# Forgetting attention with its rounds written out, four banks for transposed units, and the inverse sums in a score bank

## The reference, cut to what matters

```python
def fox_attention(q, k, v, log_f):
    c = jnp.cumsum(log_f.astype(jnp.float32), axis=1).transpose(0, 2, 1)
    ...
        s = jnp.einsum('bhqd,bhkd->bhqk', qb, kh).astype(jnp.float32) * scale
        s = s + cb[..., :, None] - c[..., None, :]
        mask = key_pos[None, :] <= q_pos[:, None]
        p = jax.nn.softmax(jnp.where(mask, s, -jnp.inf), axis=-1)
        return jnp.einsum('bhqk,bhkd->bhqd', p.astype(vh.dtype), vh)
...
    o_fox = o_fox.astype(x.dtype) * jax.nn.silu(f_gate)
```

## Time and profile before

| | |
|---|---|
| median of three runs | 1271.45 us |
| the profiled execution, its own time | 1274.48 us |
| its span in the profile | 1272.8 us |
| TensorE matmuls busy in the span | 1215.0 us (95%) |
| TensorE weight loads busy | 994.9 us (78%) |
| VectorE, ScalarE, GpSimd busy | 657.2, 547.1, 408.1 us |
| first score matmul of the forgetting stage | 733.87 us |
| first matmul of the output projection | 1088.25 us |

### The profile page before, as it was taken

How to read it: one execution, slowest core, us unless ns; L and a number is a source line. 1 busy time by engine, 2 the same in 40 slices (tenths; PEclk the granted TensorE clock), 3 DMA queues, 4 the chain that set the end, 5 groups by cost and what they waited for, 6 DMA issues and landing times. The chain is left out here.

```text
span 1272.8 us, 18800 instructions
## 1 busy us (share of the span) xinstructions
PE 1215.0 (95%) x6256; PEld 994.9 (78%) x6256; DVE 657.2 (52%) x1472; ACT 547.1 (43%) x1116; POOL 408.1 (32%) x512
## 2 busy tenths in 40 slices
PE   5999999999999999998999979999999998799997
PEld 5998877888777777777888757877787787688886
DVE  3763435101333334422555368878898897544443
ACT  5553033013444442213555357777777777211111
POOL 3554531122333333322334143153126315211110
PEclk9999999999999999999999989999999999899999
DMA  8884232223333334435444493236044201544341
GB/s 317 268 283 128 65 96 96 72 83 115 101 107 107 107 107 132 130 120 154 132 150 141 125 226 124 85 89 154 9 150 108 76 10 45 204 149 149 149 145 70
DMA packets 106819, 161.57 MB, mean 127 GB/s; under 512 B 12148, under 2 KB 62324, under 8 KB 105124
## 3 DMA queue, kind: packets, MB, share of 16 engines
q1 hardware_dynamic: 103920, 151.46, 38.4%
q10 hardware_dynamic: 2616, 8.66, 1.7%
q0 software_dynamic: 192, 0.33, 0.2%
HBM read 102.67 MB, written 57.74 MB: 126 GB/s over the span
## 5 line engine op out<-in xcount | busy, mean ns | idle before, releaser
L1038 PE MATMUL tok_tps<-h_T,tok_slot 128*128 128x512 f32 x2088 | 491.0, 393 | 0.0
L1038 PEld LDWEIGHTS tok_tps<-h_T,tok_slot 128*128 128x128 f32 x2088 | 390.4, 188 | 82.8 <-issue 2.3
L2114 PE MATMUL out_yps<-out_w,out_mix 128*128 128x512 f32 x768 | 177.2, 393 | 8.4 <-POOL out_mix L2163 7.6
L2114 PEld LDWEIGHTS out_yps<-out_w,out_mix 128*128 128x128 f32 x768 | 145.4, 190 | 40.2 <-ACT out_w L2180 8.7
L1875 ACT ACTIVATE fox_pT<-fox_tps 128x512 fp32r<-128x512 f32 x240 | 124.1, 529 | 81.7 <-PE fox_tps L1801 78.1
L1932 DVE TENSOR_TENSOR fox_pT<-fox_tps,fox_pT 128x512 fp32r<-128x512 f32 x240 | 144.3, 606 | 23.2 <-ACT fox_pT L1875 21.3
L1920 DVE TENSOR_SCALAR_CACHE_REDUCE fox_prob<-fox_sps 128x512 f32<-128x512 f32 (+1 forms) x240 | 140.8, 603 | 19.6 <-PE fox_sps L1792 15.8
L1801 PE MATMUL fox_tps<-all_ident,fox_prob 128*128 128x128 f32 x816 | 133.0, 276 | 5.3 <-ACT fox_prob L1867 3.9
L1801 PEld LDWEIGHTS fox_tps<-all_ident,fox_prob 128*128 128x128 f32 x816 | 101.6, 141 | 32.8 <-ACT fox_prob L1867 7.2
L1867 ACT ACTIVATE fox_prob<-fox_prob,fox_nm 128x512 f32<-128x512 f32 (+7 forms) x96 | 114.8, 1196 | 5.3 <-POOL fox_qb L1567 5.3
L1818 PE MATMUL fox_ops<-fox_pT,fox_v 128*128 128x512 f32 (+3 forms) x384 | 111.9, 375 | 2.0 <-ACT fox_pT L1875 2.0
(11 more groups left out here) (199 smaller groups left out, 1661.0 us busy)
## 6 DMA issues: line engine op xcount, KB each, us to landing
scr_split<-cg_stage SPq DMA_DIRECT2D x64, 256.0 KB, 2.9
open_raw<-in_w_cols SPq DMA_DIRECT2D x22, 512.0 KB, 4.3
open_raw<-in_x SPq DMA_DIRECT2D x16, 512.0 KB, 6.9
tok_xT<-in_x_cols SPq DMA_DIRECT2D x16, 512.0 KB, 6.4
scr_gates<-cg_stage SPq DMA_DIRECT2D x32, 256.0 KB, 2.5
outw_mix<-scr_mix SPq DMA_DIRECT2D x16, 512.0 KB, 4.4
out_x<-in_x SPq DMA_DIRECT2D x16, 512.0 KB, 3.5
out<-out_o ACTq DMA_DIRECT2D x15, 512.0 KB, 2.6
```

The lines of the kernel that those rows point to most:

```text
L1038: mm = nc.tensor.matmul(cps[u % 2], w[j % 2][a_][:, kk, :], hT[b_][:, kk, c * CH:(c + 1) * CH], start=(kk == 0 and r == 0), stop=(kk == KT ...
L2114: mm = nc.tensor.matmul(yps[t % 2][:, c, :], mix[t % 2][a][:, kk, :], w[b][:, kk, c * CH:(c + 1) * CH], start=(kk == 0 and n == 0), stop=( ...
```

## The change

The three rounds are written out for all engines, and the loop is gone. There are four `tps` banks, so that transposes of unit n wait for unit n-4. The bank `rps` is gone: the inverse sums are spread into `sps[0]`, the first of the two score banks. With that come two waits on TensorE. The spread waits until the last score unit in that bank, up to the end of the next turn's units, is through VectorE. The first score unit of each turn waits for SCALE of the turn whose sums were spread last (`turn` in the code is the turn being worked on; with its `max(turn - 1, 0)` all turns up to turn-2 must be copied; at turn 0 of a round all those of the round before). The order of work on the engines is otherwise the same.

```diff
-        tps = [k.ps(f"tps{b}", [P, CH]) for b in range(3)]
+        tps = [k.ps(f"tps{b}", [P, CH]) for b in range(4)]
         ops = [k.ps(f"ops{b}", [P, CH]) for b in range(2)]
-        rps = k.ps("rps", [P, CH])
+        rps = sps[0]
...
+        def starts(t):
+            return (t // n_turns) * n_scores + at_turn(t % n_turns)[0]
+
...
-        def rounds(eng, round_):
-            with eng.Fori(0, ROUNDS - 1) as r:
-                round_(r, False)
-            round_(ROUNDS - 1, True)
+        def rounds(round_):
+            for r in range(ROUNDS):
+                round_(r, r == ROUNDS - 1)
...
                         if n >= 2:
                             pe.wait_ge(negated, S.at(n - 1))
+                        if n >= QT and i == QT - 1 and c == 0:
+                            turn = next(x for x in range(n_turns + 2) if starts(x) == n) - 1
+                            pe.wait_ge(scaled, G.at(max(turn - 1, 0)))
...
                     def transposes(u, n, t, q0):
                         e, g, j, i0 = u
-                        pe.wait_ge(pt_lo, K.at(n - 2 if n >= 3 else 0))
+                        pe.wait_ge(pt_lo, K.at(n - 3 if n >= 4 else 0))
...
-                            mm = nc.tensor.transpose(tps[n % 3][:, i * P:(i + 1) * P],
+                            mm = nc.tensor.transpose(tps[n % 4][:, i * P:(i + 1) * P],
...
                         pe.wait_ge(diag_done, G.at(t + 1))
                         pe.wait_ge(scaled, G.at(t))
+                        pe.wait_ge(negated, S.at(starts(min(t + 3, n_turns + (not last))) - 1))
...
-                rounds(pe, round_)
+                rounds(round_)
```

More of the change, by code:

```diff
@@ L1768, in round_ @@
                                 second.load_values(sp, r + 1, 0, 0, NCH)
-                rounds(sp, round_)
+                rounds(round_)
             @block.tensor
@@ L1874, in pt_high @@
                         act.wait_ge(weighed, K.at(max(n - PT + 1, 0)))
-                        nc.scalar.activation(pT[n % PT][HI][:, i0 * P:CH], tps[n % 3][:, i0 * P:CH], ACT.Copy
+                        nc.scalar.activation(pT[n % PT][HI][:, i0 * P:CH], tps[n % 4][:, i0 * P:CH], ACT.Copy
                                              ).then_inc(pt_hi, 1)
@@ L1906, in _ @@
                 act.wait_ge(opening.memory_stored, 8 * ColumnUnits.TURNS)
-                rounds(act, round_)
+                rounds(round_)
             @block.vector
@@ L1931, in pt_low @@
                         dve.wait_ge(pt_hi, K.at(n + 1))
-                        nc.vector.tensor_tensor(pT[n % PT][LO][:, i0 * P:CH], tps[n % 3][:, i0 * P:CH],
+                        nc.vector.tensor_tensor(pT[n % PT][LO][:, i0 * P:CH], tps[n % 4][:, i0 * P:CH],
                                                 pT[n % PT][HI][:, i0 * P:CH].bitcast(F32), ALU.subtract
@@ L1963, in _ @@
                 round_(0, False, prologue=True)
-                rounds(dve, round_)
+                rounds(round_)
             @block.gpsimd
@@ L2015, in round_ @@
                     gated_output(n_turns - 1)
-                rounds(pool, round_)
+                rounds(round_)
     return 8 * ROUNDS * n_turns
```

## The result

The changed kernel takes 1278.29 us in the median of five runs (1277.19 to 1278.95) against 1271.45 us before: ratio 1.0044, 95% interval 1.0033 to 1.0055. It is slower, as forecast, by more than the forecast's middle (1276.0 us). The profiled execution took 1278.13 us, its span is 1276.2 us.

The account below looks back on a forecast made before the run. TensorE's own order of work was taken as the forgetting stage's bound, VectorE and ScalarE close behind. Terms -3.22 + 7.76 + 0 = +4.5 us on the 1271.45 us median gave 1276.0 us; forecast's own range 1274.0 to 1278.5, overall 1269.0 to 1282.0.

Parts of the forecast that it names:

- the jump back: Loop's return from round 0 to 1: boundary takes 33.11 us against 29.89 without a jump, so writing out saves 3.22 us.
- register arithmetic: Loop's register work for the waits: turn 1 to 2 takes 21.89 us looped, 21.91 written out, so removal counts 0.
- waits for SCALE inside the rounds: First score of turns 2 to 7 waits for SCALE of the turn before; delays add up to 2.26 us a round.
- waits for SCALE at two boundaries: First score of the next round's turn 0 waits for SCALE of turn 7: 0.54 us later at each of two boundaries.
- the spread's wait: Spread matmuls wait until VectorE is through the next turn's scores in the shared bank; long over by then, so 0.
- the fourth bank: Removes TensorE's 0.42 us wait once a round for a transposed bank; counted 0, since the new wait ends later.
- the end of SCALE plus 0.06 us: Start of a turn's first score after SCALE; 0.06 us is the gap from ScalarE's copy to a waiting weighing.
- the third score decides: In turns 2 and 3 the third score already waited for VectorE, so only +0.65 and +0.51 us of delay survive.
- Absorption: Rival: TensorE's start delays vanish within each turn; full gives 1268.2 us (chance 0.14), partial 1271.7 us (0.18).
- The clock: Rival: new idle times in turns 2 and 3 drop TensorE to half clock, six falls giving 1282 us; chance 0.12.
- The stall that stays: Rival: longer written-out code stalls at the first boundary as the jump did, giving 1279.2 us; chance 0.04.

## Why the prediction was right

*The place and the mechanism* were right: the first score of a turn stands for SCALE, what is left of the delay at the end of a turn is not caught up again, and the jump's gain doesn't cover it. In turns 4 to 6 the delay of TensorE's first score lasts in full, as forecast (0.60, 0.60 and 0.32 us later in the kernel with the wait alone, and SCALE 0.60, 0.61 and 0.31 us). In turns 2 and 3 VectorE decides how much of it is left. Term by term:

| term | forecast | measured |
|---|---|---|
| the jump back | -3.22 | -3.29 (33.11 to 29.82) |
| the rest of the loop (register arithmetic in the forecast) | 0 (far end -0.8) | -0.87 |
| waits for SCALE inside the rounds | +6.48 | +7.05 |
| waits for SCALE at two boundaries | +1.28 | +1.7 |
| the spread's wait, the fourth bank | 0 | 0 |
| sum | +4.5 | +4.6; from first to last SCALE +4.8 |

The forecast's third and fourth rows together are the 7.76 us (2.16 us a round without turn 7, and 0.54 + 0.10 at each boundary); the measured ones are the wait's kernel less the rounds written out alone.

Two terms were mis-sized, and against each other, so that the sum comes within 0.1 us of the measured one is in part luck. The waits were 1.0 us dearer than forecast, the loop's removal 0.9 us better.

The first is the step "the end of SCALE plus 0.06 us". It is 0.14 to 0.15 us in every trace that has this wait: I had taken the gap from another pair of operations, a weighing after ScalarE's copy. By turns, measured against forecast:

- Turns 4, 5 and 6 measured 0.60, 0.61 and 0.31 us for 0.38, 0.39 and 0.23. The gap gives 0.08 of each, which is all of turn 6. In turns 4 and 5 another 0.13 and 0.11 come from my choice of the round: in rounds 0 and 1 TensorE's first score was late by itself. Round 2 showed 0.51 in turn 4 and 0.50 in turn 5, and with the loop gone all rounds are like it.
- The boundaries measured 0.87 us each for 0.64; the gap counts twice in it, for turn 7 and for turn 0.
- Turns 2 and 3 came out lower, 0.50 and 0.35 us for 0.65 and 0.51. Here the step "the third score decides" failed. That score did come 0.70 and 0.56 us late, but at the sixth score only 0.49 and 0.38 us were left. VectorE had been late by itself, and its own delay (0.48 and 0.33 us in the rows above) is what lasted.

The second is the step "register arithmetic is worth nothing". I had read it between SCALE of turns 1 and 2, where it is nothing, and not between those of turns 2 and 4, where it is 0.6 us in round 0. The -0.87 is what all of the loop but its jump cost; that the registers are the reason is not shown.

Two smaller readings: the 0.42 us wait for the third bank stands at the start of turn 4, where rows 7 have it, and not of turn 3. And the forecast's waits of 0.2 to 0.5 us in turns 4 to 6 were 0.92 us in turn 4, since the fourth bank's 0.42 went into it, 0.50 in turn 5, and none listed in turn 6.

*The rivals.* Absorption: 2.3 us a round stay (83.8 against 81.5 us, the same in every round to 0.04 us), so the rival is refuted as a whole. In part it is right: of the delays of the first scores in turns 2 and 3 about two thirds vanish, where the forecast had counted on a good half. A new wait is absorbed where one already stood, which the second bank shows too. The 22 per cent that the weight loads' busy share leaves free were not free for these waits. The Trainium skill ("Trainium Kernel Development and Optimization", Performance Expectations) offers that share as a measure of how close a kernel is to roofline; here it did not tell how much added waiting the stage can take. The clock: waits of up to 1.22 us left it at 1.00 in every round of both profiles, so that rival is refuted inside the rounds. The stall that stays: refuted by the rounds written out alone. The Trainium skill ("Runtime: NRT & Kernel Launch", Instruction fetch mechanics) says that a taken branch can force a fetch before execution goes on; the trace agrees so far as the 2.43 us without an instruction on ScalarE are gone with the branch.

*The distance of the medians.* The first comparison gave +6.8 us, the repeat +5.0 by its ratio (0.0039 x 1272.8) and +4.6 by its medians. The stage's own stretch gives +4.8, and with the fallen clock +6.1. The interval of the first ratio reaches from +4.2 to +7.0 us, so the forecast's 4.5 lies in it. Whether falls of the clock make some of the first comparison's 6.8 us was not tested run by run.

What stays open: why the loop makes rounds 0 and 1 longer, and unequally (0.61 and 0.26 us), nearly all of it between SCALE of turns 2 and 4. No kernel took the registers away and left the loop. How much each of the three causes leaves in the kernel with SCALE ahead of LOW, and what made the clock fall once, are open too.

## What to carry to other kernels

When two uses are to share a bank, look at what reads it last and what TensorE wants to write next: here the second score bank costs 0.1 us at each boundary and the first one some 9 us in all, with the same work and the same kinds of wait. A new wait is free where the engine already stands for something that ends later. Where it doesn't, ask which engine decides there. In turn 3 it was VectorE, and of TensorE's 1.47 us no more than VectorE's own 0.33 us lasted; in turn 4 it was TensorE, and its whole 0.60 us did. Undo a change's parts one by one before it is thrown away: the loop's removal was worth 3.8 us and the fourth bank 1.7 us (once the sums were in the second score bank), and the choice of the first score bank hid both. Moving an operation ahead delays the one that it passes: SCALE ahead of LOW gave back only about half.

## What the runs showed that I had not expected

- A jump back of a hardware loop costs 3.3 us here: ScalarE is 2.4 us without instructions and TensorE waits 2.2 us. The remaining 1.1 us fit the half clock that follows, but no run took the clock apart from the wait.
- From the end of ScalarE's copy to the first score matmul it is 0.14 to 0.15 us, in all four kernels with that wait on the first score.
- With SCALE ahead of LOW, VectorE's sum waits 0.81 us for LOW, and TensorE's third score 0.23 us for VectorE, though no engine has more work.
- A fourth bank takes away a wait of 0.35 us in the trace and shortens the turns by 0.7: the wait listed in front of one instruction is not all that a buffer gives.
